# Forgetting attention by pairs of heads with the key gate in the score product, and modulation slabs streamed past column tiles of TensorE

## The reference, cut to what matters

```python
def forgetting_attention(q, k, v, f_logit, b_f):          # 8 heads of 64, 4 blocks of 128 queries
    log_f = jax.nn.log_sigmoid(f_logit + b_f)
    c = jnp.cumsum(log_f, axis=1).transpose(0, 2, 1)
    ...
        logits = (jnp.einsum('bhqd,bhkd->bhqk', qb, k) * scale
                  + cb[..., None] - c[:, :, None, :])
        logits = jnp.where(key_pos[None, :] <= q_pos[:, None], logits, -jnp.inf)
        p = jax.nn.softmax(logits, axis=-1)
        return jnp.einsum('bhqk,bhkd->bhqd', p.astype(v.dtype), v)

# in each of the two hybrid layers
    shift, scale, gate = jnp.split(sc @ w_mod + b_mod, 3, axis=-1)         # sc: 1024, w_mod: 1024 x 3072
    shift_c, scale_c, gate_c = jnp.split(scc @ w_mod + b_mod, 3, axis=-1)
```

## Time and the profile before

| | |
|---|---|
| median of 3 runs | 3563.17 us (3560.43 to 3567.79) |
| the profiled execution | 3562.43 us, span 3560.7 us |
| PE busy | 3338.7 us (94%) |
| DVE, ACT, POOL busy | 1522.0, 1175.3, 66.1 us |
| mean granted TensorE clock | 0.941 of full speed |

### The profile page before, as it was taken

How to read it: one execution, slowest core, us unless ns; L and a number is a source line. 1 busy time by engine, 2 the same in 40 slices (tenths; PEclk the granted TensorE clock), 3 DMA queues, 4 the chain that set the end, 5 groups by cost and what they waited for, 6 DMA issues and landing times.

```text
span 3560.7 us, 39937 instructions
## 1 busy us (share of the span) xinstructions
PE 3338.7 (94%) x16164; PEld 2637.3 (74%) x16164; DVE 1522.0 (43%) x2158; ACT 1175.3 (33%) x1905; POOL 66.1 (2%) x114
## 2 busy tenths in 40 slices
PE   8999999998899998998999989988989899989887
PEld 6878887683578886876888668857867687668565
DVE  4535444335454544356242642143334634442343
ACT  4234323222342324136242531143222624331332
POOL 1000000000000000000000000000000000000100
PEclk9899999895799998999999989999989999999998
DMA  4332222230132221110111011211111022021211
GB/s 156 110 115 97 102 96 95 93 114 0 37 119 105 106 89 42 54 42 19 62 60 54 1 47 53 95 39 53 47 54 65 19 84 73 18 77 60 92 66 65
DMA packets 40939, 246.96 MB, mean 69 GB/s; under 512 B 5432, under 2 KB 5696, under 8 KB 16864
## 3 DMA queue, kind: packets, MB, share of 16 engines
q1 hardware_dynamic: 30384, 204.78, 16.3%
q0 software_dynamic: 10416, 40.22, 3.4%
HBM read 240.78 MB, written 4.19 MB: 69 GB/s over the span
## 4 chain that ended last, share of the span: by engine, by line
PE 85%; DVE 8%; ACT 4%; issue 2%; DMA 1%; SPq 0%; DVEq 0%; ACTq 0%; POOLq 0%
PE PS L673 14%; PE PS L674 14%; PE PS L675 14%; PE PS L653 7%; PE PS L652 7%; PE PS L654 7%; PE PS L617 2%; PE PS L619 2%; PE PS L618 2%; PE PS L554 2%; PE PS L571 1%; PE PS L1015 1%; DVE SMALL L1953 1%; PE PS L1042 1%; PE PS L813 1%
## 5 line engine op out<-in xcount | busy, mean ns | idle before, releaser
L673 PE MATMUL PS<-HHX,WHX 128*128 128x512 f32 (+1 forms) x1632 | 586.4, 359 | 60.5 <-DVE WLM L1809 31.0
L674 PE MATMUL PS<-HL,WHX 128*128 128x512 f32 (+1 forms) x1632 | 584.4, 358 | 0.0
L673 PEld LDWEIGHTS PS<-HHX,WHX 128*128 128x128 f32 x1632 | 316.7, 194 | 116.6 <-issue 44.5
L1270 ACT ACTIVATE WHX<-W 128x2048 fp32r<-128x2048 f32 x108 | 186.1, 1723 | 637.3 <-DMA W<-in_w 406.3
L675 PE MATMUL PS<-HHX,WLX 128*128 128x512 f32 (+1 forms) x1056 | 372.9, 353 | 0.0
L674 PEld LDWEIGHTS PS<-HL,WHX 128*128 128x128 f32 x1632 | 315.7, 193 | 42.5
L1809 DVE TENSOR_TENSOR WLX<-W,WHX 128x2048 fp32r<-128x2048 f32 x60 | 137.5, 2292 | 351.3 <-ACT WHX L1270 351.2
L652 PE MATMUL PS<-HH,WH 128*128 128x512 f32 x704 | 277.9, 395 | 1.4 <-DVE HL L1547 1.4
L653 PE MATMUL PS<-HL,WH 128*128 128x512 f32 x704 | 279.0, 396 | 0.0
L654 PE MATMUL PS<-HH,WL 128*128 128x512 f32 x704 | 275.6, 392 | 0.0
L1809 DVE TENSOR_TENSOR WL<-W,WH 128x2048 fp32r<-128x2048 f32 x68 | 155.9, 2292 | 267.6 <-ACT WH L1270 267.6
(11 more groups left out here) (365 smaller groups left out, 6004.6 us busy)
## 6 DMA issues: line engine op xcount, KB each, us to landing
W<-in_w SPq DMA_DIRECT2D x172, 1024.0 KB, 4.7
XC<-in_wm POOLq DMA_DIRECT2D x12, 1024.0 KB, 5.1
H<-in_wm POOLq DMA_DIRECT2D x12, 1024.0 KB, 5.6
W<-in_wb SPq DMA_DIRECT2D x24, 512.0 KB, 3.3
W<-in_w SPq DMA_DIRECT2D x8, 768.0 KB, 4.1
PR<-in_nbias POOLq DMA_DIRECT2D x12, 256.0 KB, 2.9
ARENA<-in_nbias POOLq DMA_DIRECT2D x12, 256.0 KB, 2.9
X<-in_x SPq DMA_DIRECT2D x2, 1024.0 KB, 6.4
```

What stands on the lines that cost most here:

```text
L673: pe.matmul(dst, wh[:, s, c], hi[:, k, t0:t1], start=k == 0, stop=False)
L674: pe.matmul(dst, wh[:, s, c], lo[:, k, t0:t1], start=False, stop=False)
L1270: act.activation(dst[:, s, 0:n], W[:, s, 0:n], ACT.Copy).then_inc(wh_ready[s], 1)
```

## The change

Two parts. **Modulation:** SC (2 columns) is now the stationary operand and the slab moves past it, 8 matmuls of 256 columns for one slab; the four k tiles of a half go to four groups of columns of the array (outputs at partitions 0, 32, 64, 96 of bank 4 or 5). ACT copies the 128x256 result to MODP (`act_mod`, new in the stages' ACT functions), and with the next slab PE adds the four groups and turns the result by a matmul with a constant (`pe_mod_sum`). MODP shares memory with the masks MFWD and MBWD, which POOL makes later. **Attention:** 16 jobs of two heads. FQ and FK have 8 head tiles of 128 rows: 64 rows of q or k, 8 rows that pick the head and hold the gate's sum, zeros in the rest; the score product gives q k - c_k in one (c_q falls away under the softmax), and a matmul with FIDENT and FCAUS adds the causal mask. DVE takes both heads' maxima in one reduce, ACT the exponentials from PSUM. Values are multiplied for each job with the transposed probabilities stationary; DVE divides the output, PE turns it (`turn`). The split of OY is done inside the stage. POOL clears FQ and FK and fills in the gate's rows at `foxgate`.

```diff
@@ pe_mod
             pe.wait_ge(mod_loaded[i % 2], 16 * (i // 2 + 1))
-            for m in range(2):
-                c = 4 * i + 2 * m
-                for k in range(KT):
-                    mm = pe.matmul(PS[:, 5, c:c + 2], mod_slab(i)[:, k, m * P:(m + 1) * P], SC[:, k, :],
-                                   start=k == 0, stop=k == KT - 1)
+            wait(pe, sem("mod_out"), i - 1)
+            for half in range(2):
+                for g in range(4):
+                    k = 4 * half + g
+                    mm = pe.matmul(PS[32 * g:32 * g + 2, 4 + i % 2, 0:SLAB], SC[:, k, :], mod_slab(i)[:, k, :],
+                                   start=half == 0, stop=half == 1, skip_group_check=True)
             mm.then_inc(mod_used, 1)
+            if i:
+                pe_mod_sum(pe, i - 1)
+
+    def pe_mod_sum(pe, i):
+
+        pe.wait_ge(sem("mod_out"), i + 1)
+        ones = PC[:, PCOL["mod_sum"]:PCOL["mod_sum"] + 2]
+        for m in range(2):
+            c = SLAB + 4 * i + 2 * m
+            mm = pe.matmul(PS[:, 4 + i % 2, c:c + 2], MODP[:, m * P:(m + 1) * P], ones, start=True,
+                           stop=True, skip_group_check=True)
+        mm.then_inc(sem("mod_summed"), 1)
+
+    def act_mod(act, st, n, done=0):
+
+        for i in range(st["mod"] + done, st["mod"] + done + n):
+            act.wait_ge(mod_used, i + 1)
+            wait(act, sem("mod_summed"), i)
+            act.activation(MODP[:, :], PS[:, 4 + i % 2, 0:SLAB], ACT.Copy).then_inc(sem("mod_out"), 1)
...
@@ act_norm, behind the reciprocal root
+        if st.prev and st.prev.kind == "units" and st.prev.mods - st.prev.lead == len(st.prev.evs):
+            act_mod(act, st.prev, 1, st.prev.mods - 1)
+        act_mod(act, st, st.mods)
...
@@ pe_fox: scores, values, turn
+            for hh in range(2):
+                pe.matmul(PS[:, p + hh, 0:nk], FQ[:, 2 * t + hh, nk - P:nk], FK[:, 2 * t + hh, 0:nk], start=True,
+                          stop=False, skip_group_check=True)
+                mm = pe.matmul(PS[:, p + hh, nk - P:nk], FIDENT[:, :], FCAUS[:, :], start=False, stop=True,
+                               skip_group_check=True)
...
+                    mm = pe.matmul(PS[:, 6, hh * 64:hh * 64 + 64], FAT[:, n % 2, o:o + P], FV[:, kb, c:c + 64],
+                                   start=kb == 0, stop=kb == j["qb"], skip_group_check=True)
...
+        for n in range(nj + 2):
+            if n + 2 < nj:
+                scores(jobs[n + 2])
+            if 0 <= n - 1 < nj:
+                values(jobs[n - 1])
+            if n < nj:
+                transposes(jobs[n])
+            if 0 <= n - 2 < nj and jobs[n - 2]["last"]:
+                turn(jobs[n - 2])
...
@@ act_fox
+        act_split(act, st.split_next, 0, 0)
+        exps(jobs[0])
+        for n in range(nj):
+            if n + 1 < nj:
+                exps(jobs[n + 1])
+            evac(jobs[n])
+            if n == 1:
+                act_split(act, st.split_next, 0, 1)
+            if n in (3, 5, 7, 9):
+                split((n - 3) // 2)
...
@@ dve_fox
+            dve.tensor_reduce(SMALL[:, p:p + 2], PS[:, p:p + 2, 0:nk], AX, ALU.max,
+                              negate=True).then_inc(sem("fox_max"), 1)
...
@@ pe_foxgate: the gate logits at partitions 0 and 64
-            mm = pe.matmul(PS[0:8, 6, :], WFS[:, k, :], H[:, k, 0:T], start=k == 0, stop=k == KT - 1)
+            for p0 in (0, 64):
+                mm = pe.matmul(PS[p0:p0 + 8, 6, :], WFS[:, k, :], H[:, k, 0:T], start=k == 0, stop=k == KT - 1,
+                               skip_group_check=True)
...
@@ POOL at foxgate
+                pool.memset(FQ[:, :, :], 0.0).then_inc(sem("fox_pad"), 1)
+                pool.memset(FK[:, :, :], 0.0).then_inc(sem("fox_pad"), 1)
...
+                for hh, v in ((0, FQ[64:128, 0:8:2, :]), (1, FQ[0:64, 1:8:2, :])):
+                    pool.wait_ge(sem("fox_pad"), 2 + hh)
+                    pool.affine_select(out=v, in_=v, compare_op=ALU.not_equal, fill=1.0, base=-hh,
+                                       pattern=[[-2, 4], [0, T]], channel_multiplier=1).then_inc(sem("fox_pad"), 1)
```

More of the change, by code:

```diff
@@ L143, in tok @@
             evs=evs, nt=nt, **kw)
[L145 to L163, removed]
     norm("H", "load", "mix0_norm")
@@ L181, in plan_stages @@
             norm("H", "down", "mix1_norm", mods=1)
-            add("foxgate", {**full(6, 7), **free(6, 7)}, mods=1)
+            add("foxgate", {**full(6), **free(6)}, mods=1)
             units(["u", "q", "k"], at="H", era="odd", split=True, first=True, mods=3)
@@ L185, in plan_stages @@
             add("sgu", {**full(0, 1, 2, 3), **free(0, 1, 2, 3)})
[L186 to L192, removed]
+            jobs = [dict(n=4 * t + qb, t=t, qb=qb, nk=P * (qb + 1), last=qb == 3) for t in range(4) for qb in range(4)]
+            add("fox", {**full(0, 2, n=8), **free(0, 2, n=8), **full(4, n=16), **free(4, n=16), **full(7, n=4),
+                        **free(7, n=4)}, jobs=jobs)
+            assert base["mod"] == MODS_EVEN
             units(["res", "res"], at="Y", era="odd", split=True, first=True, final=True, mods=2)
@@ L768, in pe_attn @@
-        pe.wait_ge(freed[7], st["free", 7])
-        for b in range(6):
-            wait_free(pe, st, b, 0)
-        ahead = 2
-        for j in jobs[:ahead]:
-            scores(j)
-        mod = 0
-        for j in jobs:
-            if j["n"] + ahead < len(jobs):
-                scores(jobs[j["n"] + ahead])
-            if st.mods * (j["n"] + 1) // len(jobs) > mod:
-                pe_mod(pe, st, 1, mod)
-                mod += 1
-            transposes(j)
-            if j["last"]:
-                values(j)
+            n, t = j["n"], j["t"]
@@ L785, in na_tiles @@
+        scores(jobs[0])
+        scores(jobs[1])
+        for n in range(nj + 2):
[7 more added lines that the diff above has]
+                turn(jobs[n - 2])
     def na_tiles(n):
@@ L1117, in act_units @@
     def act_units(act, own, st):
-        if st.first:
+        if st.first and st.at != "Y":
             act_split_first(act, st)
@@ new lines, in post, with low @@
+        def post(j):
+            t = j["t"]
+            dve.wait_ge(full[7], st["full", 7] + t + 1)
+            dve.tensor_copy(OY[:, 4 + t, :], PS[:, 7, :]).then_inc(freed[7], 1)
+        def low(k):
+            dve.wait_ge(hh_ready, st.split_next["hl"] + k + 1)
+            dve.tensor_tensor(OYL[:, k, :], OY[:, k, :], HHOY[:, k, :].bitcast(F32),
+                              ALU.subtract).then_inc(hl_ready, 1)
+        dve_mod_save(dve, 0, MODS_EVEN - 1)
+        maxima(jobs[0])
+        dve_split(dve, st.split_next, 0, 0)
@@ new lines, in dve_fox @@
+        maxima(jobs[1])
+        for n in range(nj + 3):
+            if n + 2 < nj:
+                maxima(jobs[n + 2])
+            if 0 <= n - 1 < nj:
+                divide(jobs[n - 1])
+            if 0 <= n - 3 < nj and jobs[n - 3]["last"]:
+                post(jobs[n - 3])
+            if n == 2:
+                dve_split(dve, st.split_next, 0, 1)
+            if n in (4, 6, 8, 10):
+                low((n - 4) // 2)
+            if n in (11, 13, 15):
+                low(4 + (n - 11) // 2)
@@ L1940, in dve_da @@
+        low(7)
     def dve_da(dve, own, st):
@@ L2367, in _ @@
     def _(pe):
-        pe.wait_ge(consts, 9)
+        pe.wait_ge(consts, 7)
         for st in stages:
```

308 lines of the change are left out of this document (166 added, 142 removed).

## The result

The changed kernel takes 3453.48 us (median of 4 runs, 3448.9 to 3455.79), the kernel before 3561.8 (4 runs, 3551.4 to 3567.79): ratio 0.9697, 95% interval 0.9672 to 0.9722. The forecast was 3453. The total came out by more than the steps did: three of them were off by 4 to 5 us, in both directions, and 4.7 us came from stages that nobody touched.

A forecast was written before the change was run, and what follows sets the result against it. The prediction took PE as the bound, busy 94% of the span, with the attention mostly at half clock. Its terms summed to 108.8 us off the profiled 3562.4, giving 3453 us; range 3430 to 3496.

The forecast's parts named there:

- two slabs in lru: Recurrence stage: PE waits for ACT's copy of the first slab before the gate products, a loss of 5 us.
- behind cp: Slab behind unit cp: shorter slab and half-clock stretch removed, 2.9 + 2.6 = 5.5 us gained.
- three ahead of the even `res`: Three slabs ahead of the first `res` units: 3 us gained, between 0 and 5.
- `foxgate`: Slab at the forgetting attention's gate: 0 gained, since PE waits there for DVE's H.
- behind u, q, k, g: Four open slabs: each falls from 3.63 to 1.5 us and regains 1.7 us of clock.
- behind v, and spatial gating: Slab saves 2.1 us; gating starts at full clock, three tiles save 6.2; together 8.2 us.
- attention: From the end of gating to the first unit: 63.5 us against 130.5, PE still the bound; 67 us gained.
- norm behind the attention's layer: Slab ahead of it no longer holds back L571, but ACT makes two copies on the path; 1.3 us gained.
- six slabs at `down`: Time given back mostly waited for at DVE's hidden tiles; 6 us gained in all.
- the slab in the open: Slab not hidden by waits: 1.5 us instead of 3.63, with the clock expected to hold behind it.
- the rival: Attention stays at half clock: 110 us in place of 63.5, whole kernel 3500 us; chance 12%.
- Hidden: ... POOL's clearing and selecting: At the attention's gate: some 25 us of POOL from 650, not needed before unit q's end, so no cost.

The follow-up runs named there:

- run 2: Changed kernel with all eight matmuls of a modulation slab in one group of columns instead of four: 3463.63 us, ratio 0.9731.
- run 8: Changed kernel with every value product of the attention issued twice: 3476.55 us, ratio 0.9764.
- runs 9 to 11: Changed kernel, score products over 8 rows (3510.99 us) or 64 (3512.8 us); kernel before, gate and score products over 128 rows (3541.26 us).
- run 12: Kernel before with gate and score products over 128 rows and value products writing 128 columns: 3542.07 us, ratio 0.9959.
- run 3: Changed kernel with POOL clearing FQ and FK only behind the gate's running sum, not beside it: 3456.26 us, ratio 0.9711.
- run 6: Changed kernel with ACT copying the first slab in lru ahead of `act_prep`, not behind it: 3453.98 us, ratio 0.9692.

## Why the prediction was right, and where it was not

Terms in us gained; measured is the shift between the same instructions of PE in the two profiled timelines.

| term | forecast | measured |
|---|---|---|
| two slabs in lru | -5 | -5.4 |
| behind cp | 5.5 | 1.6 |
| behind vb | 3.8 | 3.6 |
| three ahead of the even `res` | 3 | 3.6 |
| `foxgate` | 0 | -4.9 |
| behind u, q, k, g | 15.2 | 14.1 |
| behind v, and spatial gating | 8.2 | 8.4 |
| attention | 67 | 72.0 |
| behind the first odd `res` | 3.8 | 3.6 (and 0.5 on the way) |
| norm behind the attention's layer | 1.3 | 1.9 |
| six slabs at `down` | 6 | 5.2 |
| all behind the odd feed-forward part | 0 | 4.7 |
| sum | 108.8 | 108.9 |

**Right by its reasons:** the slab in the open (1.44 us, clock held; run 2 shows that four groups make it), the start of the gate products in lru to 0.1 us, a pair of heads at 12.31 us, and a PE that is the bound (run 8). For the clock the forecast said that part of the array was unused in each product; for the scores and the gate runs 9 to 11 show that, for the values' 64 columns run 12 shows nothing of it. Had the clock stayed low, the attention would be 111 us (the rival said 110, counted from the end of gating, 1.4 us earlier) and the kernel 3511 to 3513. The rival said 3500, and both lie beyond the 3496 at which the stated range ended.

One reason was incomplete. The forecast took the clock from differential attention, whose scores use 64 rows too and which keeps 1.00; it did not say why they do no harm there. The trace of the kernel before has a row on it:

```profile
1605.03 1.13 PE L804 MATMUL PS<-ARENA 64*128 64x256 f32 x8
```

One behind the other they would need 8 x 0.21 = 1.7 us; they take 1.13. The code alternates between rows 0 to 63 and rows 64 to 127, and the products of the two halves run at once and fill the rows together; the old forgetting attention took one head, and so one half of the rows, at a time. That this keeps the clock up in differential attention is inferred; no run tests it.

**The step that failed** is the line "Hidden: ... POOL's clearing and selecting". I asked when its result is needed and not what it shares while it runs. The trace shows what: 6.27 us for a step of 0.42, and 4.9 lost. The Trainium skill says so in "SBUF — State Buffer", section Who interferes with whom: a `tensor_scalar` that takes both of VectorE's ports shares one pair with GpSimd and stands for the whole of the other's instruction. By that page the step waits for what is left of the first clearing (643.83 + 3.53 - 644.82 = 2.5 us). The trace agrees and shows more: the step waits for the second clearing (3.5 us) as well, whose row starts at 647.28, 0.08 before the first one's ends. That makes 6.1 of the 6.27 us. The page gives the ports to whoever was issued first and would let the step go between the two; here the measurement decides. The step takes 0.42 us alone for 512 columns, where the two-input L1938 takes 0.69; that fits the use of both ports, though no row names the ports. The page says too that a VectorE instruction with two inputs in SBUF stands only against a GpSimd instruction that reads; here L1881 takes 4.88 us for 8 beside the clearing of run 3, 0.61 each, and 2.47 for 4 without one in the changed kernel, 0.62: it agrees again.

**Mis-sized terms.** Behind cp 1.6 in place of 5.5. The term let PE go on as soon as the slab was done; but the unit behind it needs the low parts of its weights, which DVE makes behind its copies. Before:

```profile
109.13 4.36 PE L554 MATMUL PS<-SC,XC 128*128 128x2 f32 x32
110.30 2.28 DVE L1809 TENSOR_TENSOR WLX<-W,WHE 128x2048 fp32r<-128x2048 f32 x1
113.35 0.77 PE L673 MATMUL PS<-HHE,WHE 128*128 128x512 f32 x1
```

And after:

```profile
114.56 1.04 PE L545 MATMUL PS<-XC,SC 128*2 128x256 f32 x16
115.53 0.61 PE L557 MATMUL PS<-PC,MASKS 128*128 128x2 f32 x4
117.95 0.50 PE L700 MATMUL PS<-HHE,WHE 128*128 128x512 f32 x1 [1.81 <-DVE WLX L1871]
```

The low parts were ready 3.45 us behind the slab's start (112.58) and the slab of 4.36 us hid them; now they are ready after 3.3 us and PE stands for them. The half-clock stretch, counted as removed, came at 118.6 to 122.0 all the same. The late end of the lru stage is not the cause: in run 6 it ends 5 us sooner, and the wait at this place is 1.83 us with the clock at 0.66 in the 5 us behind it. Attention 72.0 in place of 67: of 14.1 us for stalls, start, end and a first window at half clock, 9.4 were needed (58.6 from the end of gating, less 4 x 12.31); no window at half clock came in this execution, while that of run 3 had two.

**The 4.7 us behind the odd feed-forward part** are clock too, where both kernels issue the same work behind the same wait. The place where most of it arises, before and after:

```profile
3303.92 0.79 PE L673 MATMUL PS<-HHX,WHX 128*128 128x512 f32 x1 [2.98 <-DVE WLX L1809]
3304.00:3312.00 8.00, 8.00 (x23) 6.29 (x24) 1.90 (x1) 3.19 (x2) 3.38 (x7) 0.62 0.59 210
```

```profile
3199.19 0.50 PE L700 MATMUL PS<-HHX,WHX 128*128 128x512 f32 x1 [2.98 <-DVE WLX L1871]
3199.00:3207.00 8.00, 7.81 (x34) 6.49 (x35) 2.43 (x2) 3.80 (x3) 3.74 (x7) 1.00 0.76 255
```

In 8 us PE gets through 23 matmuls in the one and 34 in the other, and the shift between the two timelines grows by some 3 us there. The change does nothing at this place, so this gain is luck.

**Open:** what decides where a half-clock stretch falls. Such stretches are of the size of the spread between runs of one kernel (7 us here, 16 before). That the forecast met the total to 1 us is in part luck: -4 (cp) and -5 (`foxgate`) stand against +5 (attention) and these 4.7.

## What to carry to other kernels

Price a clock and the work it runs together: here 19 and 18 us alone were 72 together, and what brought the clock was to let the score products use all 128 rows and not 64, though 56 of them hold zeros. For an operation "hidden" on GpSimd, ask which VectorE instruction runs beside it and through which ports, and put it behind the one on the critical chain. A saving of 5 us on the path of a kernel that falls to half clock now and then may not be seen: look for it at the next stages' clock before you drop the mechanism.

## What was unexpected of the hardware

- GpSimd's selection, which reads SBUF, took 6.90 us in the changed kernel beside VectorE's splits of HL and of the weights (two inputs in SBUF), and 1.09 in run 2, where it ran after them; before the change 4.10. So the shared ports cost either side.
- Busy time did not tell the clock. With 64 rows PE was busy for 108.8 of 111.3 us at 0.52; with one job in flight for 54.2 of 74.1 at 0.98. The Trainium skill, "TensorE: Matmul & The Clock Gate", section What's actually happening, has the clock set by how busy the engine has been; these two runs, taken as the trace counts busy time, go against it, and the measurement decides.
- The same 353 instructions took 57.1 to 57.2 us at five starts (776.3 to 804.2), 60.2 at 783.7 and 64.3 at 781.0.
